# Moving the products of the modulation units from GpSimd to ScalarE in a four-layer transformer kernel

## What is computed

```python
shift, scale, gate = jnp.split(s_lat @ w_mod[layer] + b_mod[layer], 3, axis=-1)   # layers 0 and 1
x_in = x * (1.0 + scale[:, None, :]) + shift[:, None, :]
...
shift, scale, gate = jnp.split(c_act @ w_ada[l] + b_ada[l], 3, axis=-1)           # layers 2 and 3
x = x + gate[:, None, :] * y
```

## Time and profile before

| | before |
|---|---|
| time, median of three runs | 2783.09 us |
| the profiled execution's own time | 2779.19 us |
| its span, first to last instruction | 2777.3 us |
| TensorE matmul busy | 2665.5 us (96%) |
| VectorE busy | 1635.5 us (59%) |
| ScalarE busy | 1196.5 us (43%) |
| GpSimd busy | 1664.1 us (60%) |
| mean granted TensorE clock | 0.98 |

### The profile page before, as it was taken

The page is one execution under the profiler, slowest core; times in us unless marked ns, Lnnn a source line. Parts: engine busy times, 40 slices in busy tenths (PEclk is TensorE's granted clock), DMA queues, the critical chain, the costliest instruction groups (busy, mean ns, idle before and its releaser), DMA issues.

```text
span 2777.3 us, 49264 instructions
## 1 busy us (share of the span) xinstructions
PE 2665.5 (96%) x21271; PEld 2442.3 (88%) x21271; DVE 1635.5 (59%) x1911; ACT 1196.5 (43%) x1418; POOL 1664.1 (60%) x874
## 2 busy tenths in 40 slices
PE   5999999999999999999999969999999899999999
PEld 4888898888889899889999959999789789998799
DVE  3353444654445558686676666764875557656863
ACT  1244444343443334444585354632454446334443
POOL 0067777987777789998557623065778440557600
PEclk9999999999999999999999979999999999999999
DMA  9999998997888997776556826755567656655565
GB/s 340 336 284 269 264 262 252 280 274 234 241 241 250 310 276 228 226 226 194 150 159 193 214 83 185 191 151 152 189 184 221 168 172 171 174 145 167 181 169 152
DMA packets 819960, 594.10 MB, mean 214 GB/s; under 512 B 22038, under 2 KB 740256, under 8 KB 819232
## 3 DMA queue, kind: packets, MB, share of 16 engines
q1 hardware_dynamic: 815632, 576.53, 71.8%
q10 hardware_dynamic: 4112, 14.42, 1.3%
HBM read 583.82 MB, written 6.95 MB: 213 GB/s over the span
## 4 chain that ended last, share of the span: by engine, by line
PE 73%; POOL 12%; DVE 7%; DMA 5%; ACT 1%; issue 1%; SPq 1%; POOLq 0%; DVEq 0%; ACTq 0%
PE G L2493 46%; POOL ring L848 7%; PE G L2512 4%; POOL mod_rows L856 3%; POOL ring L855 2%; PE G L2394 2%; DMA ring<-in_w_ada_dram 2%; PE A L2444 2%; DVE ring_r L1521 2%; PE A L2575 1%; PE A L2581 1%; PE A L2407 1%; PE A L2578 1%; PE G L2739 1%; DMA ring<-in_w_mod_dram 1%
## 5 line engine op out<-in xcount | busy, mean ns | idle before, releaser
L848 POOL TENSOR_SCALAR ring<-ring,act_in 128x512 f32<-128x512 f32 x448 | 956.5, 2146 | 932.3 <-DMA ring<-in_w_ada_dram 720.3
L2493 PE MATMUL G<-H_r,ring_r 128*128 128x256 f32 x8720 | 1463.6, 286 | 29.6 <-DVE S_r L1510 20.7
L2493 PEld LDWEIGHTS G<-H_r,ring_r 128*128 128x128 f32 x8720 | 1273.5, 191 | 57.1 <-issue 48.7
L1521 DVE TENSOR_TENSOR ring_r<-ring,ring_r 128x2048 fp32r<-128x2048 f32 x334 | 808.1, 2422 | 257.0 <-ACT ring_r L889 255.9
L889 ACT ACTIVATE ring_r<-ring 128x2048 fp32r<-128x2048 f32 x334 | 638.8, 1913 | 397.2 <-DMA ring<-in_a_w_out_dram 81.3
L2493 PE MATMUL G<-M_r,ring_r 128*128 128x256 f32 x4176 | 733.0, 283 | 0.3 <-DVE ring_r L1521 0.3
L2493 PEld LDWEIGHTS G<-M_r,ring_r 128*128 128x128 f32 x4176 | 595.4, 189 | 9.4 <-issue 8.2
L2493 PE MATMUL G<-S_r,ring_r 128*128 128x256 f32 x1536 | 437.5, 285 | 0.0
L856 POOL TENSOR_TENSOR mod_rows<-mod_rows,ring 128x512 f32<-128x512 f32 x196 | 331.1, 1689 | 15.4
L855 POOL TENSOR_TENSOR ring<-ring 128x512 f32<-128x512 f32 x196 | 328.6, 1677 | 16.3
L2493 PEld LDWEIGHTS G<-S_r,ring_r 128*128 128x128 f32 x1536 | 296.0, 193 | 0.1
(11 more groups left out here) (476 smaller groups left out, 2853.9 us busy)
## 6 DMA issues: line engine op xcount, KB each, us to landing
ring<-in_w_in_dram SPq DMA_DIRECT2D x120, 1024.0 KB, 5.7
ring<-in_w_ada_dram SPq DMA_DIRECT2D x192, 512.0 KB, 6.0
ring<-in_a_w_in_dram SPq DMA_DIRECT2D x86, 1024.0 KB, 7.3
const<-in_w_mod_dram SPq DMA_DIRECT2D x192, 256.0 KB, 4.6
ring<-in_c_w_in_dram SPq DMA_DIRECT2D x48, 1024.0 KB, 5.8
ring<-in_w_mod_dram SPq DMA_DIRECT2D x16, 2048.0 KB, 13.0
ring<-in_a_w_out_dram SPq DMA_DIRECT2D x32, 1024.0 KB, 6.9
ring<-in_w_out_dram SPq DMA_DIRECT2D x32, 1024.0 KB, 5.9
```

The source lines that it names most:

```text
L848: g.mark(pool.tensor_scalar(w[:, i, :], w[:, i, :], act_in[:, k, c:c + 1], None, ALU.mult))
L1521: v.tensor_tensor(w_low(tl), w_raw(tl), w_up(tl).bitcast(F32), ALU.subtract).then_inc(w_lo, 1)
L2493: ins = pe.matmul(G[tl.bank][:, 0:SEQ], w, x, start=(k == 0 and n_ == 0), stop=(k == KT - 1 and n_ == 2))
```

## The change

ScalarE multiplies each GpSimd unit in place, directly behind the rounding of a tile, with an ACTIVATE Copy whose scale is the activation column; the units that `load(q - 1)` has loaded are multiplied in `upper(q)`. GpSimd waits for the two products (`pool_mul`) in place of the DMA and only adds. The transposes of the totals (`MOD_COLS_AT`) move about one tile later.

```diff
 for _p in range(len(POOL_BLOCKS)):
-    _q = POOL_TILE[8 * (_p // 2) + 7] - 1
+    _q = POOL_TILE[8 * (_p // 2) + 7]
...
+        pool_mul = sem("pool_mul")
...
             for n in range(len(POOL_BLOCKS) // 2):
-                c = 0 if POOL_BLOCKS[2 * n][0] < 2 else 2
                 total = mod_rows[n % 2][:, :]
                 for u in range(8):
                     m = 8 * n + u
                     w = pool_unit(m)
-                    pool.wait_ge(pool_full[m % 2], 16 * (m // 2 + 1))
-                    for i in range(2):
-                        k = 2 * u + i
-                        g.mark(pool.tensor_scalar(w[:, i, :], w[:, i, :], act_in[:, k, c:c + 1], None, ALU.mult))
-                    g.settle()
+                    pool.wait_ge(pool_mul, 2 * m + 2)
...
                     act.activation(w_up(tl), w_raw(tl), ACT.Copy).then_inc(w_hi, 1)
+                for m in range(pool_units_by(q - 2), pool_units_by(q - 1)):
+                    c = 0 if POOL_BLOCKS[2 * (m // 8)][0] < 2 else 2
+                    act.wait_ge(pool_full[m % 2], 16 * (m // 2 + 1))
+                    for i in range(2):
+                        k = 2 * (m % 8) + i
+                        w = pool_unit(m)[:, i, :]
+                        act.activation(w, w, ACT.Copy, scale=act_in[:, k, c:c + 1]).then_inc(pool_mul, 1)
```

## The result

The changed kernel takes 2808.72 us (median of four runs, 2804.78 to 2811.24), the kernel before beside it 2780.86. The ratio is 1.0098, 95% interval 1.0079 to 1.0117: 27 us slower. The forecast was 2773, 10 us faster, with a range from 2760 to 2792; the result lies outside it. The profiled execution has a span of 2809.4 us, 32.1 more than the one of before.

What follows compares the result with a forecast made beforehand. TensorE, busy 2665.5 of 2777.3 us, was taken to bound the kernel, leaving its stalls and half clocks to win. Terms: -14.8 + 5.2 = -9.6 us, giving 2769.6 for the profiled execution, 2773 on the median; range 2760 to 2792.

Steps and rivals of the forecast that it cites:

- Part 1: Products leave GpSimd, which ceases to set the pace at five places where TensorE waits: 14.8 us won.
- 3.1 us at L2474: TensorE's wait for GpSimd's total at 2144 us; with its half clock, 4.8 us won.
- 1.8 us of L2726: TensorE's wait for ScalarE behind a rounding whose tile landed late: 1.8 us won.
- L2549: TensorE's wait of 5.8 us at 542 us, for squares slowed beside GpSimd and a late tile: 2.3 us won.
- The wait of L1510: Three waits, 3.3 us, for input splits whose VectorE share GpSimd slows: half, 1.6 us, won.
- Part 2: ScalarE multiplies, 1.35 us a unit, mostly covered; exposed at three places: 5.2 us lost, 6.8 at the upper bounds.
- 2.5 us at L2559: Loss at 194 us, a read behind a rounding that waits for a saturated DMA; 1.35 to 3.8 possible.
- other two terms of 1.35 us: Losses where ScalarE is on the way to a stall: L2474 at 950 us and L3053 at 2051 us.
- (b): Rival: slower, ScalarE's order exposes products in the attentions, 46 us fully, 23 half (2796); chance 0.19 with (c).
- Part 3: SyncE's load loop through ScalarE, 13.5 to 15.4 us, fits two units nearly everywhere; lateness hidden except at 542 us.
- (a): Rival: no measurable change, stalls shrink only to the next late thing, VectorE's queue and DMAs: 2780; chance 0.33.
- (c): Rival: function tables reloaded for Copy on ScalarE, 224 times; given almost nothing, within (b)'s 0.19.

Runs made afterwards that it cites:

- e1: The kernel before with the 448 products left out on every engine, so GpSimd only adds: 2765.18 us, ratio 0.9959.
- e12: The kernel before with only the transposes of the totals moved one tile later: 2781.35 us, ratio 1.0004.
- e5: The changed kernel with GpSimd issuing its units' DMAs itself, so SyncE does not wait for products or adds: 2781.76 us, ratio 1.0011.
- e6: The kernel of e5 with each product cut to 2 columns, the rest of the unit unscaled: 2774.36 us, ratio 0.9975.
- e7: The changed kernel, SyncE loading, but ScalarE multiplies in upper(q) the units that load(q) has loaded, one tile earlier: 2781.51 us, ratio 1.0001.
- e3: The changed kernel with each product cut from 512 to 2 columns, the rest of the unit unscaled: 2785.43 us, ratio 1.0024.
- e4: The kernel before with GpSimd issuing its units' DMAs itself, still doing its own products: 2826.95 us, ratio 1.0188.
- e8: The kernel of e5 with the products behind the chain's steps of the tile's first half, where there are such steps: 2774.68 us, ratio 0.9981.
- e10: The kernel of e7 with the products behind the chain's steps of the tile's first half: 2766.97 us, ratio 0.9943.
- e9: The kernel of e5 with GpSimd multiplying the 91 units loaded in cx_in, s_in2 and s_in3, ScalarE the other 133: 2773.72 us, ratio 0.9979.
- e11: The kernel of e7 with GpSimd multiplying the units loaded in cx_in, s_in2 and s_in3: 2764.62 us, ratio 0.9934.

## Why the prediction was wrong

**Part 1 was right, as far as it can be tested.** Forecast 14.8 us for a GpSimd without products; e1 gives 11, interval 7 to 16. Of its places, the waits of 2.6 us at L2671 and of 3.1 us at L2474 and the 1.8 us of L2726 are all gone in e1, and L2549 falls from 5.8 to 4.4, a gain of 1.4 for the 2.3 forecast. The wait of L1510 did not shrink: 3.3 us became 5.6 in e1. In the changed kernel only the first two are gone; at 541 us the 5.8 have become 4.3 for a low part and, behind it, 3.1 for the squares (both in the waits above), and L2726 stands longer than before. The 3.1 us of L2474 were put down to the change as a gain of its own; e12 removes that wait alone and shows no gain on the whole. So the total came out, and not each term of it.

**Part 2 had the right durations and a price that was probably too low, for places that were mostly others.** 1.35 us a unit was forecast and 1.32 measured; forecast exposure 5.2 us (6.8 at most), measured 10 by e5 against e6 (7 by the medians), with 4 to 16 as its bounds, so that 5.2 is not excluded. Its largest term, 2.5 us at L2559, was not one: that wait grows from 3.8 us to 5.6 in the changed kernel, but e1, without any products, has 5.4 there. Of the other two terms of 1.35 us, the wait at 2051 us is 1.4 in e5 and 0.9 in e6, and the one at 950 us is in neither. What it missed is the attention of `cx_in`: it was given as rival (b), with 46 us at full exposure for 34 units and a fifth as the limit. There e5 loses 6.3 us more than e6, about a quarter of the 24 us that the 18 units of `cx_in` would cost. The upper end of the range, 2792, was not worked out from any term; (b) at half exposure gave 2796.

**Part 3 is the step that failed.** It was priced at nothing: the little lateness that it found, in `ax_in`, was to stay hidden except at 542 us. The runs say 24 us (after against e5; e7 against after 27). The loop was closed at the wrong point: it was drawn from a load through landing, rounding, products and adds to the load after the next, 13.5 to 15.4 us, and held against two units, 17 to 18 us. But the loop isn't paced by landings. ScalarE comes to a unit when TensorE has ended a tile, at the start of a turn, since it reads the finished tile first and works in order. The right sum starts there: read and gap 0.3, rounding 1.9, products 1.2, adds 4.5 with one held up, the rest between them, and the unit's issue 0.4: 8.6 us, to be held against one turn, 5.9 us by 1258.0 and 1263.93. It is over by 2.7 us there, and that is how late the load at 1266.61 is. With two free adds the same sum is 6.7 us, still over a turn of 5.9 but not over one of 6.9, the median turn of the changed kernel; how much of the 24 us the held adds cost was not tested. Between turns whose unit isn't due, and where the chain's steps make a turn longer, SyncE catches up. One tile earlier there are two turns, 11.8 us, for the same 8.6, and the loss is gone (e7).

The prediction even said that SyncE's waits might be more, but took it that they would "end before TensorE needs the tile". That rested on an average rate; the late loads come one by one, most of them directly behind the unit of the tile before (67 of 83).

The product's 1.32 us therefore cost twice. With it taken away the time falls by 21 us inside the loop (e3) and by 10 outside (e6).

By the ratios the way from the kernel before to the changed one divides so: freed GpSimd -11, GpSimd behind ScalarE and with its own issues +4 (e6 against e1), products' time in ScalarE's order +10, SyncE's loop +24, together +27. The steps are differences of successive kernels, so that they give the whole is no test of them. Each has an uncertainty of 4 to 6 us, and the +4 can't be told from nothing.

**The rivals.** (a) named an exclusion of VectorE and GpSimd at nearly every unit, by the Trainium skill, SBUF — State Buffer, section Who interferes with whom. The rows show such a hold of one add, 3.23 for 1.30 us at 1262.94, but the adds' mean is 1.71 us after (1826 and 1587 ns) and 1.68 before; the collision moved and on average didn't grow. It did fall on the late loads (3.7 us for two adds, above), so (a)'s mechanism had a part in the lateness, though not as the hold at nearly every unit that was feared. VectorE's subtraction fell from 2422 ns to 2345 by its group's total, 782.8 us for 808.1, so it did profit as forecast. (b) had the right sign, for a minor part. (c), table reloads, did not come: the profile has no table load at the line of the products, and those of the other lines are as many as before (43 at L905 as at L902).

By the estimate that was worked out from the Trainium skill, GPSIMD Engine Reference, section Engine selection, GpSimd would be freed of 291 us. It was freed of 940 (1664.1 to 724.0); the rows had it right.

What was not among the rivals is that the time would be lost in SyncE's queue although GpSimd was busy less than half as long. The forecast's own test for (a), "SyncE's L747 waits with a tile landing later than before", is what came true, at a size of its own.

## What to carry to other kernels

When work on a buffer moves to an engine that runs in step with the main loop, the buffer's turnaround is no longer the sum of the operations: it starts where that engine comes to it in its program. Count it from the start of the turn to the release, and hold it against the number of turns until another in-order queue needs it; if it doesn't fit, try doing the work a turn earlier before giving up the idea. An average utilisation of an engine doesn't answer this, nor does its being freed.

## What the runs showed of the hardware

- A DMA issue takes 0.77 us of GpSimd's time (e4), and one of SyncE's 0.37. Kernels with GpSimd's own loads came out 10 to 13 us behind their like with SyncE's loads (e8 against e10, e9 against e11), but e5 and e7 are only 3 apart; what that is was not settled.
- A wait of 1.8 us in front of L2726 left TensorE's granted clock at 1.00 before the change; with 2.6 us at the same place it was 0.50 afterwards, the 1.2 GHz level, for at least the 4 us shown above. By the matmul count the stretch from 1188 to 1395 us lost 3.0 us in all, where e5, without the late load, won 3.8. The length of the wait alone is not what decides: in the changed kernel a wait of 1.9 us at 980 us left the clock at 1.00 (980.5 to 984), and one of 1.9 us at 1095 us left it at 0.57 (1096 to 1100).
